# Opening of the second part, first layer's rates and modulation blocks rearranged in a fused two-model kernel

## The reference, cut to what matters

```python
# first block: 512 tokens, width 1024, two layers
for l in range(2):
    proj = rms_norm(h, g_mix[l]) @ w_in[l]          # q, k, v, xr, gr
    h = h + concat([diff_attention, rg_lru * gelu(gr)]) @ w_out[l]
    h = h + square(relu(rms_norm(h, g_mlp[l]) @ w_mlp_in[l])) @ w_mlp_out[l]
    h = h + sigmoid(rms_norm(h, g_ple[l]) @ w_ple_gate[l]) * (p[l] @ w_ple_proj[l])
x = rms_norm(h, g_final)
# rg_lru needs softplus(-lru_lambda), 512 values ("rates")

# second block: 256 context tokens ahead of the 512
for i in range(2):
    sh, scl, gt = split(silu(c) @ mod_w[i] + mod_b[i])      # "modulation"
    u = rmsnorm(h, norm_w[i]) * (1 + scl) + sh
    z, xbc, dt = split(u @ in_w)                            # i = 0: mamba
    xbc = silu(conv5(xbc) + conv_b)                         # five taps
    dt = softplus(dt + dt_bias)                             # "rates" of the heads
    ...                                                     # 8 groups, then attention
```

## Time and profile before

| | us |
|---|---|
| median of 3 runs | 2604.95 |
| lowest and highest | 2599.8, 2607.89 |
| the profiled execution, its own time | 2605.17 |
| its span (first to last instruction) | 2603.3 |
| PE busy | 2441.3 (94%) |
| PEld busy | 2055.2 (79%) |
| DVE busy | 1446.5 (56%) |
| POOL busy | 1298.7 (50%) |
| ACT busy | 805.6 (31%) |

### The profile page before, as it was taken

The page is one execution under the profiler, slowest core; times in us unless marked ns, Lnnn a source line. Parts: engine busy times, 40 slices in busy tenths (PEclk is TensorE's granted clock), DMA queues, the critical chain, the costliest instruction groups (busy, mean ns, idle before and its releaser), DMA issues.

```text
span 2603.3 us, 36232 instructions
## 1 busy us (share of the span) xinstructions
PE 2441.3 (94%) x13506; PEld 2055.2 (79%) x13506; DVE 1446.5 (56%) x1785; ACT 805.6 (31%) x1724; POOL 1298.7 (50%) x1204
## 2 busy tenths in 40 slices
PE   7989999999999999999987999999999988998997
PEld 5767888888766788888876898898898887876786
DVE  7974211134776531111357688788788786227762
ACT  2343111112233420011233433333333432335771
POOL 6735766677774376666754234434444341362003
PEclk9999999999999999999988999999999997899999
DMA  4211344433221033444232111101101120121001
GB/s 154 81 49 49 121 138 138 140 120 105 85 77 65 33 113 129 139 138 130 97 104 81 33 49 42 55 32 48 48 32 48 48 97 27 33 81 49 1 2 49
DMA packets 33690, 199.30 MB, mean 77 GB/s; under 512 B 4400, under 2 KB 6576, under 8 KB 13616
## 3 DMA queue, kind: packets, MB, share of 16 engines
q1 hardware_dynamic: 22896, 159.93, 18.0%
q10 hardware_dynamic: 10688, 37.83, 4.4%
HBM read 192.50 MB, written 5.24 MB: 76 GB/s over the span
## 4 chain that ended last, share of the span: by engine, by line
PE 74%; DVE 16%; issue 5%; ACT 3%; POOL 1%; DMA 0%; DVEq 0%; ACTq 0%; SPq 0%; POOLq 0%
PE ps L407 36%; PE ps L697 11%; PE ps L934 5%; DVE convd L2069 3%; PE ps L815 2%; PE ps L515 2%; PE ps L793 1%; POOL wlo L363 1%; DVE xc L1770 1%; PE ps L832 1%; PE ps L1015 1%; PE ps L434 1%; PE ps L1032 1%; DVE convd L2083 1%; PE ps L624 1%
## 5 line engine op out<-in xcount | busy, mean ns | idle before, releaser
L359 POOL TENSOR_SCALAR whi<-wraw 128x512 fp32r<-128x512 f32 x584 | 399.8, 712 | 1260.9 <-PE ps L697 539.4
L363 POOL TENSOR_TENSOR wlo<-wraw,whi 128x512 fp32r<-128x512 f32 x584 | 869.3, 1518 | 0.0
L407 PE MATMUL ps<-uhi,whi 128*128 128x512 f32 x896 | 357.7, 399 | 24.5 <-DVE ulo L1721 18.1
L407 PE MATMUL ps<-uhi,wlo 128*128 128x512 f32 x896 | 351.2, 392 | 0.0
L407 PE MATMUL ps<-ulo,whi 128*128 128x512 f32 x896 | 350.5, 391 | 0.0
L697 PE MATMUL ps<-inhi,whi 128*128 128x384 f32 (+1 forms) x784 | 249.2, 353 | 24.8 <-ACT raw L1377 18.1
L697 PE MATMUL ps<-inlo,whi 128*128 128x384 f32 (+1 forms) x784 | 237.8, 338 | 0.0
L697 PE MATMUL ps<-inhi,wlo 128*128 128x384 f32 (+1 forms) x784 | 237.8, 338 | 0.0
L407 PEld LDWEIGHTS ps<-uhi,whi 128*128 128x128 f32 x896 | 169.6, 189 | 68.2 <-issue 24.9
L1890 DVE TENSOR_TENSOR h<-h,ps 128x1024 f32<-128x1024 f32 x40 | 48.8, 1221 | 307.8 <-PE ps L407 307.8
L407 PE MATMUL ps<-hidhi,whi 128*128 128x512 f32 x512 | 202.2, 395 | 0.0
(11 more groups left out here) (425 smaller groups left out, 4798.1 us busy)
## 6 DMA issues: line engine op xcount, KB each, us to landing
wraw<-in_wstream SPq DMA_DIRECT2D x150, 1024.0 KB, 4.8
modraw<-in_modw ACTq DMA_DIRECT2D x48, 512.0 KB, 3.5
hspill<-hres ACTq DMA_DIRECT2D x1, 3072.0 KB, 8.7
hback<-hspill ACTq DMA_DIRECT2D x1, 3072.0 KB, 9.8
h<-in_x ACTq DMA_DIRECT2D x2, 1024.0 KB, 5.0
out<-hfin SPq DMA_DIRECT2D x2, 1024.0 KB, 3.9
gw<-in_gates ACTq DMA_DIRECT2D x2, 512.0 KB, 5.2
pT<-in_pT ACTq DMA_DIRECT2D x2, 512.0 KB, 5.3
```

The lines of the kernel that those rows point to most:

```text
L359: pool.tensor_scalar(whi[:, s, c], wraw[:, s, c], 1.0, 0.0, ALU.mult, ALU.add).then_inc(wraw_read, 1)
L363: ins = pool.tensor_tensor(wlo[:, s, c], wraw[:, s, c], whi[:, s, c].bitcast(F32), ALU.subtract)
L407: mm = pe.matmul(ps[:, 2 * bank + m, :], a[:, w, c:c + P], b[:, kb, :], start=(n == 0 and i == 0), stop=(n == KB - 1 and i == 2))
```

## The change

It has three parts.

1. In the first layer, both halves of the rates move. On ACT `lru_rates(0)` follows the rounding and the squares. On DVE only the four-wide bias step (`gate_bias`) stays ahead of `ulo`; the softplus follows `add_squares`, and its last three steps (`rate_ends`) follow `lambdas`.
2. A modulation block is 256 columns wide: 12 blocks in a layer instead of 24, each with the same eight matmuls, two turns, and 1 MB of weights a fetch. The fetch of the next layer's gate weights and ACT's half of its rates move from the end of MLP chunk 1 to that of chunk 2, since `modraw` now covers their place.
3. In the second part's opening, the context's sum moves into gate tile 2, after its first 12 matmuls; the eight small loads are issued ahead of `norm_root(3)`; the sums of `hsqr` are made by eight matmuls with the two columns as the stationary operand and 512 columns moving, into four column groups (so that PSUM bank 5 is cleared first), copied by ACT to `srow` and turned by four small matmuls; DVE begins on the first four of the eight spread rows; ACT copies the context's high halves in two pieces around the square root; `turn_dt` runs before `T_XS0`; ACT's exponential of `arow` runs first; the first tap of each of the four blocks runs on ACT (`first_copy`) right after its copy; DVE makes the five dt steps after block 1, then blocks 2 and 3.

```diff
-MODS = 3 * D // P
+MODW = 2 * P
+MODS = 3 * D // MODW
-    modraw = at("modraw", 184, [P, KB, P])
+    modraw = at("modraw", 184, [P, KB, MODW])
+    srow = at("srow", 136, [P, S])
...
-                    mm = pe.matmul(ps[32 * j:32 * j + 2, 5, 0:P], cvec[:, kb, :], modraw[:, kb, :],
+                    mm = pe.matmul(ps[32 * j:32 * j + 2, 5, 0:MODW], cvec[:, kb, :], modraw[:, kb, :],
...
-            pe.matmul(ps[:, 4, 0:2], modrow[:, :], misc[:, 4:6], start=True, stop=True).then_inc(L["mod_T"], 1)
+            for n in range(2):
+                mm = pe.matmul(ps[:, 4, 2 * n:2 * n + 2], modrow[:, n * P:(n + 1) * P], misc[:, 4:6], start=True, stop=True)
+            mm.then_inc(L["mod_T"], 1)
...
+                     midway=context_sum if j == 2 and l == DEPTH - 1 else None)
...
-            for c in range(4):
-                mm = pe.matmul(ps[:, 5, 2 * c:2 * c + 2], hsqr[:, b, c * P:(c + 1) * P], gf2[:, b, :],
-                               start=(b == 0 and c == 0), stop=(b == KB - 1), skip_group_check=True)
+            j = 32 * (b % 4)
+            mm = pe.matmul(ps[j:j + 2, 5, :], gf2[:, b, :], hsqr[:, b, :], start=(b < 4), stop=(b >= 4))
         mm.then_inc(n_ss, 1)
+        pe.wait_ge(L["mod_row"], DEPTH * PER["mod_row"] + 1)
+        for c in range(4):
+            mm = pe.matmul(ps[:, 4, 2 * c:2 * c + 2], srow[:, c * P:(c + 1) * P], misc[:, 4:6], start=True, stop=True)
+        mm.then_inc(L["mod_T"], 1)
...
+        turn_dt()
         wait_split(T_XS0)
         dense(T_XS0 % 2, lambda i: i * TM, P, IN, EIGHT, False, 2, None)
-        turn_dt()
         dense(T_XS0 % 2, lambda i: i * TM + P, P, IN, EIGHT, True, 0, lambda: pe.wait_ge(dt_d, 1))
...
             if l == 0:
-                lru_rates(0)
...
                 for j in range(4):
                     next_squared(j)
+                lru_rates(0)
...
-            norm_root(3)
             if l == DEPTH - 1:
                 act.wait_ge(L["ulo_r"], DEPTH * PER["ulo_r"])
                 act.dma_start(hres[:, :, 0:CTX], io["ctx"]).then_inc(ldc, 16)
...
+            norm_root(3)
...
-        A(inhi[:, :, 0:CTX], ctxn[:, :, :], ACT.Copy).then_inc(ctx_hi, 1)
+        act.wait_ge(n_ss, 2)
+        A(srow[:, :], ps[:, 5, :], ACT.Copy).then_inc(L["mod_row"], 1)
+        A(inhi[:, 0:4, 0:CTX], ctxn[:, 0:4, :], ACT.Copy).then_inc(ctx_hi, 1)
         act.wait_ge(n_w, 1)
         A(dcol[:, 8:16], dcol[:, 0:8], ACT.Sqrt).then_inc(n_rt, 1)
+        A(inhi[:, 4:8, 0:CTX], ctxn[:, 4:8, :], ACT.Copy).then_inc(ctx_hi, 1)
...
+        def first_copy(b, blk, tile_no):
+
+            copy_in(0, b, blk, tile_no)
+            act.wait_ge(x_rd, b + 1)
+            A(convd[:, b, 0:CW], raw[b % 2][:, 0:CW], ACT.Identity, scale=cpg[:, 6 * b:6 * b + 1],
+              bias=cpg[:, 6 * b + 5:6 * b + 6]).then_inc(tap_r, 1)
...
+        act.wait_ge(ld2, 7 * 16)
+        A(arow[:, :], arow[:, :], ACT.Exp).then_inc(dt_a, 1)
         act.wait_ge(dt_d, 2)
         A(dtw[1][:, :, :], dtw[0][:, :, :], ACT.Abs).then_inc(dt_a, 1)
...
-        copy_in(0, 0, 1, None)
-        copy_in(0, 1, None, T_XS0)
+        first_copy(0, 1, None)
+        first_copy(1, None, T_XS0)
         conv_tanh(0, 0)
         conv_tanh(0, 1)
-        copy_in(0, 2, 2, None)
+        first_copy(2, 2, None)
...
-        copy_in(0, 3, None, T_BC0)
+        first_copy(3, None, T_BC0)
...
+            V.memset(ps[:, 5, :], 0.0)
+            st(V.tensor_copy(cpg[:, :], p2[:, C2_CP:C2_CP + 24]))
...
             if l == 0:
                 lambda_products(0)
-                lru_rates(0)
+                gate_bias(0)
                 for j in range(4):
                     rest(1, j, C_GMIX)
             for j in range(1, 4):
                 add_squares(1, j, sqn[j - 1])
+            if l == 0:
+                lru_rates(0)
             norm_recip(1)
...
             lambdas()
+            if l == 0:
+                rate_ends(0)
...
         context_rest(0)
-        dve.wait_ge(rb_ps, 2)
+        dve.wait_ge(rb_ps, 1)
         scaled(0)
         for b in range(KB):
             if b + 1 < KB:
                 scaled(b + 1)
+            if b == 0:
+                dve.wait_ge(rb_ps, 2)
             normed_in(b)
...
-        load_params(0, st)
-        conv(0, 0, st)
-        conv(0, 1, st)
+        def first_conv(b):
+
+            dve.wait_ge(tap_r, b + 1)
+            for n in range(1, TAPS):
+                conv_tap(b, n, st)
+
+        first_conv(0)
+        first_conv(1)
         silu(0, 0)
         silu(0, 1)
-        conv(0, 2, st)
         dve.wait_ge(dt_p, 2)
...
+        first_conv(2)
+        first_conv(3)
+        silu(0, 2)
+        silu(0, 3)
         dve.wait_ge(dt_a, 5)
...
-        conv(0, 3, st)
-        silu(0, 2)
-        silu(0, 3)
```

More of the change, by code:

```diff
@@ L133, in build @@
     misc = at("misc", 206.75, [P, 16])
-    modrow = at("modrow", 206.8125, [P, P])
+    modrow = at("modrow", 206.8125, [P, MODW])
     xc = at("xc", 136, [P, 4, S])
@@ L271, in build @@
     blk_ps = sem("block_sums")
+    tap_r = sem("first_taps")
     z_t, z_rd, x_rd, o_rd = sem("z_tanh"), sem("z_read"), sem("conv_in_read"), sem("out_read")
@@ L274, in build @@
     pre_ps, tok_r, ck_r = sem("tokens_turned"), sem("tokens_held"), sem("C_held")
-    lr_lo, lr_ps, lb_r, lb_init = (sem(n) for n in (
-        "decay_rows_lo", "decay_rows_turned", "decay_blocks", "decay_blocks_zeroed"))
+    lr_lo, lr_ps, lb_r = (sem(n) for n in ("decay_rows_lo", "decay_rows_turned", "decay_blocks"))
     xte_r, st_ps, sc_r, scan_r = sem("x_to_end"), sem("chunk_states"), sem("states_held"), sem("states_scanned")
@@ L627, in _, with context_sum @@
                 mm.then_inc(L["pp_ps"] if g < 3 else tile_done, 1)
+            def context_sum():
+                pe.wait_ge(L["acc_r"], DEPTH * PER["acc_r"] + 1)
+                pe.wait_ge(L["sqrt_r"], DEPTH * PER["sqrt_r"])
+                pe.matmul(ps[:, 4, 0:CTX], ones[:, :], ctxn[:, 0, :], start=True, stop=True).then_inc(n_ss, 1)
             for j in range(4):
@@ L632, in _ @@
                      kfree=L["u_free"] if j == 3 and l < DEPTH - 1 else None,
-                     half=L["u_free"] if j == 3 and l == DEPTH - 1 else None)
+                     half=L["u_free"] if j == 3 and l == DEPTH - 1 else None,
+                     midway=context_sum if j == 2 and l == DEPTH - 1 else None)
                 if j == 0:
@@ L636, in _ @@
                     norm_sum(3)
-                if j == 1 and l == DEPTH - 1:
-                    pe.wait_ge(L["acc_r"], DEPTH * PER["acc_r"] + 1)
-                    pe.wait_ge(L["sqrt_r"], DEPTH * PER["sqrt_r"])
-                    pe.matmul(ps[:, 4, 0:CTX], ones[:, :], ctxn[:, 0, :], start=True, stop=True).then_inc(n_ss, 1)
         def done_wait(k):
@@ L1148, in modulation @@
                     act.wait_ge(L["mod_T"], l * PER["mod_T"] + m)
-                    A(modsb[:, l * MODS + (m - 1), :], ps[:, 4, 0:2], ACT.Copy).then_inc(L["mod_ev"], 1)
+                    A(modsb[:, 2 * (l * MODS + m - 1):2 * (l * MODS + m), :].rearrange("p a b -> p (a b)"), ps[:, 4, 0:4], ACT.Copy).then_inc(L["mod_ev"], 1)
                 if 0 <= m < MODS:
                     act.wait_ge(L["mod_ps"], l * PER["mod_ps"] + m + 1)
-                    A(modrow[:, :], ps[:, 5, 0:P], ACT.Copy).then_inc(L["mod_row"], 1)
+                    A(modrow[:, :], ps[:, 5, 0:MODW], ACT.Copy).then_inc(L["mod_row"], 1)
                     if m + 1 < MODS:
@@ L1259, in _ @@
                     modulation(8 * c + 4 + j)
-                if c == 1 and l < DEPTH - 1:
+                if c == 2 and l < DEPTH - 1:
                     fetch_gates(l + 1)
@@ L1382, in conv_tanh @@
             A(raw[b % 2][:, 4 + CTX:4 + T], convd[:, b, 2 + CTX:2 + T], ACT.Tanh).then_inc(cv_t, 1)
+        act.wait_ge(ld2, 7 * 16)
+        A(arow[:, :], arow[:, :], ACT.Exp).then_inc(dt_a, 1)
         act.wait_ge(dt_d, 2)
         A(dtw[1][:, :, :], dtw[0][:, :, :], ACT.Abs).then_inc(dt_a, 1)
-        act.wait_ge(dt_a, 1)
+        act.wait_ge(dt_a, 2)
         A(dtw[1][:, :, :], dtw[1][:, :, :], ACT.Exp, scale=-1.0).then_inc(dt_a, 1)
-        A(arow[:, :], arow[:, :], ACT.Exp).then_inc(dt_a, 1)
         act.wait_ge(in_lo, KB)
@@ L1434, in group @@
             act.wait_ge(lr_ps, g + 1)
-            if not isinstance(g, int):
-                act.wait_ge(lb_init, 1)
             for r in range(HPG):
@@ L1920, in _ @@
                     lru_rates(l + 1)
+                    rate_ends(l + 1)
+                    gate_bias(l + 1)
             norm_recip(3)
@@ L1986, in make_in @@
             lo(KB - 1)
-        dve.wait_ge(n_ss, 2)
-        sums = ps[:, 5, 0:8].rearrange("p (c n) -> p n c", n=2)
+        dve.wait_ge(L["mod_T"], DEPTH * PER["mod_T"] + 1)
+        sums = ps[:, 4, 0:8].rearrange("p (c n) -> p n c", n=2)
         V.tensor_scalar(dcol[:, 0:4], sums[:, 0, :], 1.0 / D, EPS, ALU.mult, ALU.add)
@@ L1998, in context_rest @@
         def context_rest(j):
-            dve.wait_ge(ctx_hi, 1)
+            dve.wait_ge(ctx_hi, j + 1)
```

10 lines of the change are left out of this document (6 added, 4 removed).

## The result

The changed kernel takes 2572.06 us (median of 4 runs, 2569.67 to 2575.53), the kernel before beside it 2605.49 (2599.8 to 2607.89): a ratio of 0.9875, 95% interval 0.9858 to 0.9893. On another chip it was 2575.64 against 2605.65, a ratio of 0.9885 (0.9867 to 0.9903). The forecast was 2571, with a range of 2562 to 2585. The profiled execution of after took 2569.67 us, 35.5 less than that of before, with a span of 2567.9.

The account below looks back on a forecast made before the run. PE, busy 94% of the span, was taken as the bound, so only its own work or its waits count. Terms of 7.0, 6.0, 1.9, 2.4, 1.25 and 16.0 gave 34.5 us off 2605.2: 2571, range 2562 to 2585.

Parts of the forecast that it names:

- Part 1: First layer's start: PE begins behind POOL's first quarter at 11.1 instead of 18.1, softplus hidden in DVE's wait; 7.0 us off.
- Rival B: At the start, POOL and DVE collide over PE's first quarters, so the rates' move gives only 4 us: 2574; chance 0.12.
- Part 2: MLP modulation: 24 wide blocks at 1.53 us each cost 36.7 against 42.7 for narrow ones; 6.0 us off.
- Rival D: In the MLP, the wide passes of the four column groups run one after another, adding 61 us: 2632; chance 0.02.
- (a): Context's sum inside gate tile 2: PE ends the tile 4.0 sooner, but DVE's context norm is next; 1.9 us off.
- (b): Sums of squares in the opening: wide passes, ACT's copy and four turns take 4.0 us against 6.4; 2.4 off.
- (c): Spread rows in the opening: the first norm starts after 3.9 us instead of 5.2; 1.25 off.
- (d): From the end of `T_DT` to `z_tanh`: earlier dt turn, taps and copy start `z_tanh` at 1432.5, not 1448.50; 16.0 us off.
- rival A: In the opening, DVE's own convolution taps beside POOL set the pace, leaving 11 us from `T_DT` on: 2581; chance 0.16.
- Rival C: New PE gaps between the sums and ahead of `turn_dt` lower the clock, 1.7 us each: 2575; chance 0.07.
- Rival E: No change: what the opening gains is waited away in the groups behind it: 2600; chance 0.02.
- The signs of being wrong: PE waiting for POOL in the first 30 us, a wide block at 1.8 us or more, or 55 us from `T_DT` to `z_tanh`.

Follow-up runs that it names:

- e9_softplus2: The changed kernel with the first layer's softplus computed twice in DVE's wait before the first norm's reciprocal: 2581.55 us, ratio 0.9909 to the kernel before.
- r2_tail: The changed kernel with the clearing of `acc` and two small steps moved ahead of DVE's taps of block 3, second measurement: 2567.73 us, ratio 0.9855.
- e2_mod: The kernel before with only the 256-column modulation blocks and the moved fetch of gate weights: 2595.81 us, ratio 0.9977.
- e7_sum_between: The changed kernel with the context's sum between gate tiles 1 and 2 again: 2575.46 us, ratio 0.99 to the kernel before.
- r1_after: The changed kernel, unaltered, measured once more on another chip: 2575.64 us, ratio 0.9885 to the kernel before.

## Why the prediction was right, point by point

The time was right (1.1 us off the median, and the sum of 2570.7 is 1.0 off the profiled execution), its steps less so. Five of six terms were within 1.5 us, and the errors lie on both sides, so that part of the hit is luck.

- **Part 1, 7.0.** PE started at 11.34, forecast 11.1, behind POOL's first quarter as said: 6.8, and 7.4 at the reciprocal. That nothing waits behind it held. The softplus fitted with 0.84 to spare, forecast 1.7, out of two errors. The cover was 7.9 us and not 9.4, since `add_squares`, now beside POOL's splits, took 6.09 for 3.87 before; and the softplus took 7.0, as it had before, where twelve steps of 0.64 were put at 7.7 (it is thirteen steps, of unequal length). e9_softplus2 shows that the cover was needed but for that rest. Read at the MLP's first addition the part measured 7.7 alone, 9.2 and 8.8 in the two traces of the change, 7.3 in r2_tail, and 7.6 between the means of all traces; what goes beyond that isn't the edit's. One piece of it can be seen: before, the window from 70 to 80 us has a clock of 0.83, after none. Rival B did not occur: POOL's quarters came every 2.7 us beside DVE, as assumed, and PE did not wait for the next.
- **Part 2, 6.0.** It measured 4.8, by e2_mod and by the whole alike. A wide block with its turn costs 12.46 - 10.88 = 1.58 where 1.53 stood in the sum; 24 of them are 37.9 us, and the 42.7 for the narrow ones less 4.8. The mis-sized term was the block: eight pairs of passes and the fixed part. Rival D is dead: four groups of 256 columns do run side by side, sixteen passes in 1.04 us.
- **(a), 1.9.** It measured 1.9, and the reason was right: DVE's context norm and not PE was next. e7_sum_between splits it at the last squares: 1.05 of the 1.9 go with the sum's place inside tile 2 (1.8 less the 0.75 from ahead of it), and the rest stays with the earlier loads and DVE's new order. At `dcol` and `dtT` the 1.05 are hardly to be found (0.1 and 0.4), for the clock is full in the sums there: so (a) and (b) depend on one another, and only their sum, 3.8 for 4.3, is a safe reading.
- **(b), 2.4.** It measured 1.9. From the last squares' end to `dcol` it is 4.5, for the 4.0 that was taken and within 3.2 to 4.8. The last passes take 1.87, for 1.8. The error is the turns: eight passes take 1.86 where 0.167 each, 1.34, stood in the sum. The lower clock is only part of it, since the 0.167 came from a stretch that was itself mostly at the lower level (0.54); a pass of a turn costs more than one of L662 at either level (0.23 for 0.18 us at the lower, 0.13 for 0.10 at full clock). At full clock, in e7_sum_between, the eight take 1.05.
- **(c), 1.25.** It measured 1.33, with the first norm right behind the spread rows as said.
- **(d), 16.0.** It measured 14.6 at `z_tanh`, 51.5 us from `dtT` where 50 was forecast. Up to ACT's tap of block 3 the layout held to half a microsecond in its end (block 2's taps end 36.9 us after `dtT`, laid out 37.0; that tap ends at 38.5 for 38.8), though not at every step: `tab` came 0.9 and block 1's taps 1.5 early, and the two `silu` and five dt steps behind them took 6.6 for 5.2, as these `silu` too lay beside POOL's split (4.01 for 2.24 before). Behind it DVE's taps took 7.36 for 6.4, and what follows them 5.5 for 5. The set of block 1 took 5.56 for 6.4. So rival A's mechanism, DVE beside POOL, is there, but with 1.0 us of the 5 by which it put (d) lower; and of PE's wait for the copy 1.1 was left, forecast about 1.
- **The tail of the opening.** The forecast read the gain at `z_tanh` and let it pass through. But PE's transposes wait for DVE's last `silu` and ACT's copies (2.9 and 2.3), and 1.6 of the 14.6 are lost by the next group. A sum made at the landmark was 1.6 too good.
- **The sum.** At the landmarks: part 1 +2.2, part 2 -1.1, (b) and (c) -0.4, (d) -1.4 and group 0 -1.6, the rest of the recurrences +0.3: 32.6 at the last `z_tanh`, for 34.5. The 2.9 that make it 35.4 came behind it, by PE's clock in work that is the same. In r1_after they did not come, and its span is 31.6 under that of before. So the measured step of 30.0 to 33.4 us (by the medians on the two chips) is fitted by 32 and not by 34.5. The number lay close partly by luck: the clock gave 2.9 us in the profiled execution, and on the other chip the median is 4.6 over the forecast.
- **Rival C** named a real effect and gave it too small a place: it priced gaps at the change, 1.7 each, and the clock moves more, up to 7.6 us, in a stretch 700 us behind it.
- **Rival E** did not occur: of the 33.9 us at the first `z_tanh` 32.6 are left at the last one of the recurrences.
- **The signs of being wrong.** The wide block at 1.58 and the 51.5 us to `z_tanh` stay under their limits, 1.8 and 55. The third sign, POOL as what PE waits for in the first 30 us, did come about by its words: PE's first product waits for POOL (11.34). It was badly put, since the prediction itself has PE start behind POOL's first quarter; behind that start PE does not wait for POOL in the first 30 us.

## What to carry to other kernels

The longest wait of the bottleneck engine need not be worth anything. Before pricing it, follow the chain of the engine that is next (here DVE's convolutions, 2 us behind a wait of 17) and price what shortens that chain; then read the gain at a landmark behind the place where the chains meet again, not at the first instruction that comes earlier. When parts are measured one by one, compare the length of the stretch that the part touches, from the landmark ahead of it to the one behind it, and over several traces; the ends of the spans don't add up where the clock varies.
